# Weight rows of 136 columns, and activation tiles set 128 bytes from them modulo 256

## The chip, the cores and the metric

The kernel runs on one core of one Trainium2 chip. The metric is the time of one execution on the device in microseconds (us), the median of several executions. Of each kernel one execution was also recorded by the hardware profiler; all rows below come from that one.

## The reference

One inference step of a two-layer decoder trunk in float32, for 256 prompt tokens and 8 sample tokens (264 together), with 1024 model channels. Each layer does the following, cut to what matters here:

```python
h = rmsnorm(x, norm1)
z = h @ w_in                       # 1024 x 6400: attention, convolution, recurrence, gates
ya, yb, yc = branches(z, state)    # windowed attention, gated convolution, HGRN2 recurrence
mix = g[0] * (ya @ w_pa) + g[1] * (yb @ w_pb) + g[2] * (yc @ w_pc)
x = x + mix @ w_o                  # 1024 x 1024
h2 = rmsnorm(x, norm2)
x = x + square(relu(h2 @ w_up)) @ w_down   # 1024 x 4096 and 4096 x 1024
```

The products with `w_in`, `w_pa`, `w_pb`, `w_pc`, `w_o`, `w_up` and `w_down` read some 134 MB of weights over both layers. Shifted caches and new states are written out as well.

## The kernel before

All activations lie transposed: channels on the 128 partitions, the 264 tokens along the free dimension, one k tile for each 128 channels. An output tile of 128 channels is one **unit**: for each k tile three matmuls add up in one PSUM bank. Weights and activations are each split into a part that the type fp32r holds (`_hi`) and a rest (`_lo`), and the product of the two rests is dropped. In `unit` (line 688) a k tile is

```python
pe.matmul(out[:, 0:TOK], wh, rh, start=start and k == 0, stop=False)            # line 695
pe.matmul(out[:, 0:TOK], wh, rl, start=False, stop=False)                       # line 696
last = pe.matmul(out[:, 0:TOK], wl, rh, start=False, stop=stop and k == nk - 1) # line 697
```

`wh` and `wl` are a 128 x 128 block of `w_hi` and `w_lo`: these are the stationary operand and are loaded anew for each of the three. `rh` and `rl` are a k tile of 264 columns of `h_hi` and `h_lo` (or of `mix_hi`, `a_hi`, `y_hi` and their `_lo`), the moving operand. There are 6144 such matmuls: the units of `w_in` (stage "in"), the branches, then `w_o`, `w_up` ("up", 32 units a layer) and `w_down` ("down", 32 units a layer). An up unit goes over k tiles 0 to 7 of `h_hi`; a down unit over 8 of the 32 k tiles of `a_hi`, from k tile 0, 8, 16 or 24 on. The first 192 of the matmuls, up to about 32 us, are written out apart (lines 666 to 684) and follow the first loads.

Weights come in pairs of units by DMA from the SP queue into `raw`. ScalarE rounds a unit into `w_hi` (line 1043), VectorE subtracts into `w_lo` (line 1292); both tiles hold a ring of four units, and `w_used` tells when a slot is free. The first six splits write pieces of a pair, in runs of 128 columns (lines 1048 and 1298). VectorE and ScalarE also evacuate and norm; the attention and recurrence work of TensorE is put between units in small matmuls.

What the change touches is where tiles lie inside a partition. Tiles are laid one behind the other in the order of their declaration, each rounded up to 32 bytes. A k tile row of `w_hi` or `w_lo` has 128 x 4 = 512 bytes, a k tile of an activation 264 x 4 = 1056 bytes, which is 4 x 256 + 32. From the start of `w_hi` to that of `h_hi` are 16384 (`w_hi`) + 16384 (`w_lo`) + 8448 (`x`) = 41216 bytes, 161 x 256. Call **distance** the address of a moving k tile less that of the weight row that is used with it, modulo 256. It is then 0, 32, 64, ... 224 for k tiles 0 to 7 of `h_hi`, the same for `h_lo` (8448 bytes on, 33 x 256) and with `w_lo`. `mix_hi` and `a_hi` begin 32 further (76832 = 300 x 256 + 32 bytes from `w_hi`), so their distances run 32, 64, ... 224, 0; those of `y_hi` begin at 160.

Of the kernel before, what the change touches and what calls it, by code (L numbers as in the profile page):

```python
# [24 lines left out]
F32R = mybir.dt.float32r  # L25
# [5 lines left out]
P = 128  # L31
D_MODEL, DEPTH, PROMPT, SAMPLES, PAST = 1024, 2, 256, 8, 1024
TOK = PROMPT + SAMPLES
KT = D_MODEL // P
# [3 lines left out]
NG = len(GROUPS)  # L38
# [29 lines left out]

O_IN, O_O, O_UP, O_DN, OUTS = 0, 50, 58, 90, 98
RING = 4  # L70
PAIRS = UNITS // 2
LEVELS = [1, 2, 4, 8, 16, 32, 64, 128]

# [43 lines left out]
def slot(l, u):  # L117

    return (l * UNITS + u) % RING

# [6 lines left out]
def trunk(nc, io):  # L127
    with ExitStack() as ctx:
        def sb(name, shape, dt=F32, stack=ctx):
            return stack.enter_context(nc.sbuf_tensor(name, shape, dt))  # L130
# [3 lines left out]


        raw = sb("raw", [P, 3, KT, 2 * P])
        w_hi = sb("w_hi", [P, RING, KT, P], F32R)
        w_lo = sb("w_lo", [P, RING, KT, P], F32R)
        x = sb("x", [P, KT, TOK])
        h_hi = sb("h_hi", [P, KT, TOK], F32R)  # L140
        h_lo = sb("h_lo", [P, KT, TOK], F32R)
        consts = sb("consts", [P, NCONST])
# [13 lines left out]
        conv_in = sb("conv_in", [P, 3, 2 + PROMPT])  # L156


        with ExitStack() as early:
            gates = sb("gates", [P, N_GATE, TOK], stack=early)  # L160
            z = sb("z", [P, CT_GATE, TOK], stack=early)
            kv_tm = sb("kv_tm", [P, 2, NG, 2, P], stack=early)
            kv_s = sb("kv_s", [SAMPLES, NG, 2, P], stack=early)
            q_s = sb("q_s", [SAMPLES, NG, P], stack=early)
            kg = sb("kg", [P, 2, TOK], stack=early)
            v_tm = sb("v_tm", [P, 2, 2, P], stack=early)
            v_s = sb("v_s", [SAMPLES, 2, P], stack=early)
            o_c = sb("o_c", [P, 2, TOK], stack=early)
            y_a = sb("y_a", [P, TOK], stack=early)
            f_s = sb("f_s", [P, 2, SAMPLES], stack=early)  # L170
            state_p = sb("state_p", [P, 2, HD], stack=early)
            conv_s = sb("conv_s", [P, 3, SAMPLES, 2], stack=early)
            conv_u = sb("conv_u", [P, 3, SAMPLES], stack=early)
            conv_new = sb("conv_new", [P, 3, SAMPLES, 2], stack=early)
            q_heads = sb("q_heads", [P, NG, SAMPLES, 2], stack=early)
            sc = sb("sc", [P, NG, SAMPLES, 2], stack=early)
            pr_s = sb("pr_s", [P, NG, SAMPLES, 2], stack=early)
            s_rows = sb("s_rows", [2 * SAMPLES, NG * P + NG], stack=early)
            new_sc = sb("new_sc", [2 * SAMPLES, NG, SAMPLES], stack=early)
            s_stat = sb("s_stat", [2 * SAMPLES, 3], stack=early)  # L180
            new_pv = sb("new_pv", [P, NG, SAMPLES], stack=early)
            ya_new = sb("ya_new", [P, SAMPLES], stack=early)
            stat = sb("stat", [P, 2, 4], stack=early)
            s_att = sb("s_att", [P, 2 * P], stack=early)
            v_cache = sb("v_cache", [P, SAMPLES, NG, P], stack=early)

            with ExitStack() as s:
                cum_f = sb("cum_f", [P, 2, PROMPT], stack=s)
                suf_f = sb("suf_f", [P, 2, PROMPT], stack=s)
                q_lv = sb("q_lv", [P, 2, 2, PROMPT], stack=s)  # L190
                k_lv = sb("k_lv", [P, LV_SLOTS, 2, P], stack=s)
                att = sb("att", [P, 2, 4, P], stack=s)
                att_far = sb("att_far", [P, 2, 2, P], stack=s)
                k_tm = sb("k_tm", [P, 2, 2, P], stack=s)
                state_s = sb("state_s", [P, SAMPLES, 2, HD], stack=s)
            with ExitStack() as s:
                probs = sb("probs", [P, 2, 2, ROW_KEYS], stack=s)
                probs_t = sb("probs_t", [P, 4 * ROW_BLOCKS, P], stack=s)
            sb("shared_region", [P, 48 * P], stack=early)

            with ExitStack() as s:
                k_cache = sb("k_cache", [P, SAMPLES, NG, P], stack=s)
            y_hi = sb("y_hi", [P, BT, TOK], F32R, stack=early)
            y_lo = sb("y_lo", [P, BT, TOK], F32R, stack=early)
        with ExitStack() as s:
            sb("gates_below", [P, N_GATE, TOK], stack=s)
# [5 lines left out]
        a_lo = sb("a_lo", [P, FT, TOK], F32R)  # L212
        u_relu = sb("u_relu", [P, RING, TOK])
        a_full = sb("a_full", [P, RING, TOK])

        sample_parts = gates[:, 10:12, :].rearrange("p a t -> p (a t)")
        q_wide = sample_parts[:, 0:P].rearrange("p (a j m) -> p a j m", a=2, j=2)
# [182 lines left out]
        def raw_slot(p):  # L400

            return (p + 2) % 3 if p < U_UP // 2 else (p - U_UP // 2) % 2
# [20 lines left out]
        def raw_landings(l, p):  # L423

            slots = [raw_slot(q) for q in range(PAIRS)]
            return l * slots.count(raw_slot(p)) + slots[:p + 1].count(raw_slot(p)) - (raw_slot(p) in (raw_slot(0), raw_slot(1)))
# [222 lines left out]
        def _(pe):  # L649
# [26 lines left out]
            def unit_lo_last(u, out):  # L676

                pe.wait_ge(w_hi_ready, u + 1)
                for k in range(KT):
                    pe.matmul(out[:, 0:TOK], w_hi[:, u % RING, k, :], h_hi[:, k, :], start=k == 0, stop=False)  # L680
                    pe.matmul(out[:, 0:TOK], w_hi[:, u % RING, k, :], h_lo[:, k, :], start=False, stop=False)  # L681
# [1284 lines left out]
```

## Time and profile before

| | |
|---|---|
| median of 3 executions | 812.22 us (811.76 to 812.28) |
| span of the profiled execution, first to last instruction | 809.8 us |
| TensorE busy with matmuls | 801.3 us, 99% |
| VectorE, ScalarE, GpSimd busy | 70%, 54%, 34% |
| mean granted TensorE clock | 0.997 of full speed |
| HBM over the span | 300 GB/s |

The span of the profiled execution lies 2.4 us under the median, by the launch and the end of the program that it leaves out. "PE" is a matmul, "PEld" a weight load. A matmul's duration in a row (some 284 ns) runs from its start to its modelled end and overlaps the next one's; how fast the stream goes is read from the starts of matmuls that follow one another.

### The profile page before, as it was taken

To read this page: it belongs to the slowest core of one execution; us is meant where nothing else is said; L and a number is where in the kernel's file an instruction comes from. 1 tells how busy PE (TensorE), PEld (TensorE's weight loads), DVE (VectorE), ACT (ScalarE), POOL (GpSimd) and SP (SyncE) were. 2 spreads that over 40 slices of the span, in tenths; PEclk is the share of its full clock that TensorE was granted. 3 is DMA by queue.
4 is the path that set the end of the run, shared out by engine and by line. 5 is a ranking of instruction groups with operands and counts; after the bars stand their busy time and mean duration, and the time that the engine had idled before them with its cause. 6 is when DMAs were issued, how large, how long until landed. Compare 5 with 4: busy or idle time off the path is not lost.

```text
span 809.8 us, 17686 instructions
## 1 busy us (share of the span) xinstructions
PE 801.3 (99%) x6786; PEld 789.7 (98%) x6786; DVE 570.3 (70%) x774; ACT 439.6 (54%) x627; POOL 274.7 (34%) x246
## 2 busy tenths in 40 slices
PE   8999999999999999999999999999999999999996
PEld 8999999999999999999999999999999999999996
DVE  6978898577877665545577788966797666645552
ACT  6663667545557664444354637674455666644442
POOL 3599293055700000122149827702663000001220
PEclk9999999999999999999999999999999999999998
DMA  8797779868567688777558968986765767787751
GB/s 327 226 342 279 279 236 328 229 226 314 185 208 226 215 287 285 257 239 250 190 179 225 359 244 289 278 254 232 271 225 178 247 235 250 240 285 241 253 207 53
DMA packets 125721, 199.88 MB, mean 247 GB/s; under 512 B 19680, under 2 KB 115376, under 8 KB 118192
## 3 DMA queue, kind: packets, MB, share of 16 engines
q1 hardware_dynamic: 124368, 196.48, 72.3%
q10 hardware_dynamic: 1296, 2.61, 0.9%
q8 instruction: 39, 0.64, 0.3%
q14 instruction: 18, 0.15, 0.1%
HBM read 191.17 MB, written 51.90 MB: 300 GB/s over the span
## 4 chain that ended last, share of the span: by engine, by line
PE 98%; DVE 1%; DMA 1%; ACT 0%; DVEq 0%; ACTq 0%; issue 0%
PE main L695 29%; PE main L696 28%; PE main L697 28%; PE small L697 1%; PE small L696 1%; PE small L695 1%; PE small L711 1%; PE small L740 1%; PE small L754 1%; DMA raw<-in_w_in 1%; PE main L680 1%; PE main L681 0%; PE main L684 0%; PE small L792 0%; PE main L671 0%; PE small L928 0%
## 5 line engine op out<-in xcount | busy, mean ns | idle before, releaser
L1043 ACT ACTIVATE w_hi<-raw 128x1024 fp32r<-128x1024 f32 (+1 forms) x256 | 266.4, 1043 | 234.3 <-PE main L697 148.6
L1292 DVE TENSOR_TENSOR w_lo<-raw,w_hi 128x1024 fp32r<-128x1024 f32 (+1 forms) x256 | 340.8, 1332 | 65.5 <-ACT w_hi L1043 64.5
L695 PE MATMUL main<-h_hi,w_hi 128*128 128x264 f32 x1248 | 357.9, 287 | 0.0
L696 PE MATMUL main<-h_lo,w_hi 128*128 128x264 f32 x1248 | 354.0, 284 | 0.0
L697 PE MATMUL main<-h_hi,w_lo 128*128 128x264 f32 x1248 | 353.9, 284 | 0.0
L695 PEld LDWEIGHTS main<-h_hi,w_hi 128*128 128x128 f32 x1248 | 235.3, 189 | 3.0 <-DVE w_lo L1292 1.5
L696 PEld LDWEIGHTS main<-h_lo,w_hi 128*128 128x128 f32 x1248 | 235.5, 189 | 0.1
L697 PEld LDWEIGHTS main<-h_hi,w_lo 128*128 128x128 f32 x1248 | 234.2, 188 | 0.0
L695 PE MATMUL main<-a_hi,w_hi 128*128 128x264 f32 x512 | 145.4, 284 | 0.0
L697 PE MATMUL main<-a_hi,w_lo 128*128 128x264 f32 x512 | 145.2, 284 | 0.0
L696 PE MATMUL main<-a_lo,w_hi 128*128 128x264 f32 x512 | 145.2, 284 | 0.0
L696 PEld LDWEIGHTS main<-a_lo,w_hi 128*128 128x128 f32 x512 | 96.6, 189 | 0.0
L695 PEld LDWEIGHTS main<-a_hi,w_hi 128*128 128x128 f32 x512 | 96.5, 188 | 0.0
L697 PEld LDWEIGHTS main<-a_hi,w_lo 128*128 128x128 f32 x512 | 96.1, 188 | 0.0
L1698 POOL TENSOR_TENSOR sq_sum<-x 128x264 f32<-128x264 f32 x4 | 6.2, 1539 | 229.3 <-DVE x L1671 223.8
L1700 POOL TENSOR_TENSOR sq<-x 128x264 f32<-128x264 f32 x27 | 36.2, 1340 | 119.1 <-DVE x L1671 112.8
L1655 DVE SCALAR_TENSOR_TENSOR u_relu<-main,rstd 128x264 f32<-128x264 f32 x64 | 27.6, 431 | 33.5 <-PE main L697 32.6
L1259 ACT ACTIVATE a_full<-u_relu 128x264 f32<-128x264 f32 x64 | 27.1, 423 | 44.0 <-DVE u_relu L1655 43.4
L1323 DVE TENSOR_TENSOR gates<-main,rstd 128x264 f32<-128x264 f32 x48 | 20.5, 428 | 40.8 <-PE main L697 40.7
L1847 POOL TENSOR_TENSOR gated<-gated 128x264 f32<-128x264 f32 x14 | 18.2, 1303 | 86.5 <-DVE gated L1484 85.8
L1323 DVE TENSOR_TENSOR z<-main,rstd 128x264 f32<-128x264 f32 x52 | 22.1, 429 | 25.6 <-PE main L697 24.5
L695 PE MATMUL main<-mix_hi,w_hi 128*128 128x264 f32 x128 | 36.4, 284 | 0.0
(241 smaller groups left out, 1042.5 us busy)
## 6 DMA issues: line engine op xcount, KB each, us to landing
raw<-in_w_in SPq DMA_DIRECT2D x48, 1024.0 KB, 6.3
raw<-in_w_up SPq DMA_DIRECT2D x32, 1024.0 KB, 5.3
raw<-in_w_down SPq DMA_DIRECT2D x32, 1024.0 KB, 5.4
out_kvs<-in_cache SPq DMA_DIRECT2D x48, 512.0 KB
out_kvs<-in_cache SPq DMA_DIRECT2D x32, 496.0 KB
raw<-in_w_o SPq DMA_DIRECT2D x8, 1024.0 KB, 6.0
raw<-in_w_br SPq DMA_DIRECT2D x8, 768.0 KB, 4.8
gates<-q_scratch SPq DMA_DIRECT2D x4, 768.0 KB, 7.9
```

Of the source, the lines that this page charges most:

```text
L680: pe.matmul(out[:, 0:TOK], w_hi[:, u % RING, k, :], h_hi[:, k, :], start=k == 0, stop=False)
L695: pe.matmul(out[:, 0:TOK], wh, rh, start=start and k == 0, stop=False)
L696: pe.matmul(out[:, 0:TOK], wh, rl, start=False, stop=False)
L697: last = pe.matmul(out[:, 0:TOK], wl, rh, start=False, stop=stop and k == nk - 1)
L711: mm = pe.transpose(bank[0:n, col:col + k], src, ident[0:k, 0:k])
L1043: act.activation(w_hi[:, slot(l, u), 0:k, :], raw_of(u, k), ACT.Copy).then_inc(w_hi_ready, 1)
L1259: act.activation(a_full[:, j, :], u_relu[:, j, :], ACT.Square).then_inc(u_used, 1)
L1292: dve.tensor_tensor(w_lo[:, slot(l, u), 0:k, :], raw_of(u, k), w_hi[:, slot(l, u), 0:k, :].bitcast(F32), ALU.subtract).then_inc(w_lo_ready, 1)
L1323: dve.tensor_tensor(dst, main[bank_of(l, o)][:, 0:TOK], rstd[:, :], ALU.mult).then_inc(out_taken, 1)
L1655: dve.scalar_tensor_tensor(u_relu[:, j, :], main[bank_of(l, O_UP + j)][:, 0:TOK], 0.0, rstd[:, :], ALU.max, ALU.mult).then_inc(out_taken, 1)
L1700: step(pool.tensor_tensor(sq[:, :], x[:, k, :], x[:, k, :], ALU.mult))
L1847: step(pool.tensor_tensor(gated[:, s, 0, :], gated[:, s, 0, :], gated[:, s, 1, :], ALU.add))
```

## The change

Rows of the weight tiles get 8 columns (32 bytes) more, which nothing reads or writes: a k tile row is 544 bytes, 2 x 256 + 32, and a slot of eight is 4352 bytes, 17 x 256. Four unused tiles (`before_h`, `before_gates`, `before_y_hi`, `before_y_lo`) move the starts of `h_hi`, of `gates` (and with it `mix_hi` and `a_hi`, which begin where `gates` does or where the tile behind it does), of `y_hi` and of `y_lo`. From `w_hi` to `h_hi` are then 43392 bytes, 169 x 256 + 128; to `a_hi` 79232, 309 x 256 + 128; to `y_hi` 190080, 742 x 256 + 128. As a weight row and an activation's k tile now both step by 32 modulo 256, the distance is 128 for every k tile of every product; to the row of the next k tile it is 96. The three tiles of sample rows `kv_s`, `q_s` and `v_s` (8 partitions each) become parts of one tile at partitions 0, 64 and 32, which frees 2560 bytes a partition.

```diff
@@ -68,6 +68,7 @@
 RING = 4
+LINE = 8
@@ -134,9 +135,10 @@
         raw = sb("raw", [P, 3, KT, 2 * P])
-        w_hi = sb("w_hi", [P, RING, KT, P], F32R)
-        w_lo = sb("w_lo", [P, RING, KT, P], F32R)
+        w_hi_rows = sb("w_hi_rows", [P, RING, KT, P + LINE], F32R)
+        w_lo_rows = sb("w_lo_rows", [P, RING, KT, P + LINE], F32R)
         x = sb("x", [P, KT, TOK])
+        sb("before_h", [P, 4 * LINE])
         h_hi = sb("h_hi", [P, KT, TOK], F32R)
         h_lo = sb("h_lo", [P, KT, TOK], F32R)
@@ -156,15 +158,14 @@
+        sb("before_gates", [P, 7 * LINE])
         with ExitStack() as early:
             gates = sb("gates", [P, N_GATE, TOK], stack=early)
             z = sb("z", [P, CT_GATE, TOK], stack=early)
             kv_tm = sb("kv_tm", [P, 2, NG, 2, P], stack=early)
-            kv_s = sb("kv_s", [SAMPLES, NG, 2, P], stack=early)
-            q_s = sb("q_s", [SAMPLES, NG, P], stack=early)
+            sample_heads = sb("sample_heads", [P, NG * 2 * P], stack=early)
             kg = sb("kg", [P, 2, TOK], stack=early)
             v_tm = sb("v_tm", [P, 2, 2, P], stack=early)
-            v_s = sb("v_s", [SAMPLES, 2, P], stack=early)
@@ -200,7 +201,9 @@
+            sb("before_y_hi", [P, 4 * LINE], stack=early)
             y_hi = sb("y_hi", [P, BT, TOK], F32R, stack=early)
+            sb("before_y_lo", [P, 2 * LINE], stack=early)
             y_lo = sb("y_lo", [P, BT, TOK], F32R, stack=early)
@@ -212,6 +215,11 @@
+        w_hi, w_lo = (t[:, :, :, 0:P] for t in (w_hi_rows, w_lo_rows))
+        kv_s = sample_heads[0:SAMPLES, :].rearrange("p (g k c) -> p g k c", g=NG, k=2)
+        v_s = sample_heads[32:32 + SAMPLES, 0:2 * P].rearrange("p (a c) -> p a c", a=2)
+        q_s = sample_heads[64:64 + SAMPLES, 0:NG * P].rearrange("p (g c) -> p g c", g=NG)
```

Every engine's and queue's instructions stay the same in number and order. What differs in their shapes: the 256 splits on ScalarE and as many on VectorE, whose weight operands were one run of 1024 (or 768) columns, now go over 8 (or 6) runs of 128.

## Rows read from the trace of the kernel before

**Rows 1.** The page: engines, granted clock in 40 slices, the chain that ended last.
```profile
PE 801.3 (99%) x6786; PEld 789.7 (98%) x6786; DVE 570.3 (70%) x774; ACT 439.6 (54%) x627; POOL 274.7 (34%) x246
...
PEclk9999999999999999999999999999999999999998
...
PE 98%; DVE 1%; DMA 1%; ACT 0%; DVEq 0%; ACTq 0%; issue 0%
```

**Rows 2.** Groups by line and shape: the product's matmuls and the two splits.
```profile
L695 PE MATMUL main<-h_hi,w_hi 128*128 128x264 f32 x1248 | 357.9, 287 | 0.0
...
L697 PE MATMUL main<-h_hi,w_lo 128*128 128x264 f32 x1248 | 353.9, 284 | 0.0
...
L1292 DVE TENSOR_TENSOR w_lo<-raw,w_hi 128x1024 fp32r<-128x1024 f32 x240 | 322.5, 1345 | 65.5 <-ACT w_hi L1043 64.5 <-DVE cur L1439 0.2
L1043 ACT ACTIVATE w_hi<-raw 128x1024 fp32r<-128x1024 f32 x240 | 253.0, 1056 | 225.4 <-PE main L697 142.8 <-DMA raw<-in_w_down 50.5 <-DMA raw<-in_w_up 16.5
```

**Rows 3.** Waits of TensorE, two of five: us in total, times, longest.
```profile
PE small L654 <- DVE eps L1330: 1.5, 1, 1.5
...
PE main L671 <- DVE w_lo L1298: 0.4, 1, 0.4
```

**Rows 4.** Timeline of TensorE, one up unit: first matmul of each k tile.
```profile
230.89 0.28 PE L695 MATMUL main<-h_hi,w_hi 128*128 128x264 f32 x1
...
231.24 0.28 PE L695 MATMUL main<-h_hi,w_hi 128*128 128x264 f32 x1
...
231.61 0.29 PE L695 MATMUL main<-h_hi,w_hi 128*128 128x264 f32 x1
...
231.97 0.28 PE L695 MATMUL main<-h_hi,w_hi 128*128 128x264 f32 x1
...
232.33 0.28 PE L695 MATMUL main<-h_hi,w_hi 128*128 128x264 f32 x1
...
232.69 0.29 PE L695 MATMUL main<-h_hi,w_hi 128*128 128x264 f32 x1
...
233.06 0.28 PE L695 MATMUL main<-h_hi,w_hi 128*128 128x264 f32 x1
...
233.42 0.29 PE L695 MATMUL main<-h_hi,w_hi 128*128 128x264 f32 x1
...
233.79 0.28 PE L695 MATMUL main<-h_hi,w_hi 128*128 128x264 f32 x1
```

**Rows 5.** Timeline of TensorE: down stage of layer 0, four first matmuls and the last.
```profile
312.09 0.28 PE L695 MATMUL main<-a_hi,w_hi 128*128 128x264 f32 x1
...
314.26 0.29 PE L695 MATMUL main<-a_hi,w_hi 128*128 128x264 f32 x1
...
314.63 0.28 PE L695 MATMUL main<-a_hi,w_hi 128*128 128x264 f32 x1
...
314.98 0.28 PE L695 MATMUL main<-a_hi,w_hi 128*128 128x264 f32 x1
...
404.53 0.28 PE L695 MATMUL main<-a_hi,w_hi 128*128 128x264 f32 x1
```

**Rows 6.** Weight loads of 128 and of 64 columns, by line and shape.
```profile
L695 PEld LDWEIGHTS main<-h_hi,w_hi 128*128 128x128 f32 x1248 | 235.3, 189 | 3.0 <-DVE w_lo L1292 1.5 <-issue 0.2
...
L792 PEld LDWEIGHTS small<-probs_t,kv_tm 128*64 128x64 f32 x64 | 3.5, 137 | 0.3
```

**Rows 7.** The six splits that write runs of 128 columns: ns min/median/max.
```profile
L1048 ACT ACTIVATE w_hi<-raw x6: 617/632/1045, 5.4 to 12.8; 128x512 fp32r<-128x512 f32 x4, 128x1024 fp32r<-128x1024 f32 x2
...
L1298 DVE TENSOR_TENSOR w_lo<-raw,w_hi x6: 677/1155/1231, 6.0 to 15.5; 128x512 fp32r<-128x512 f32 x4, 128x1024 fp32r<-128x1024 f32 x2
```

**Rows 8.** Busy time by window: us, engine busy (x instructions), clock, DMA.
```profile
core 0: us, PE busy (x) PEld busy (x) DVE busy (x) ACT busy (x) POOL busy (x), PEclk, DMA share, GB/s
100.00:120.00 20.00, 20.00 (x167) 19.50 (x167) 19.93 (x20) 12.32 (x17) 19.60 (x13) 1.00 0.77 243
```

## The prediction

> **What bounds the kernel now.** I looked first for idle time of TensorE. There is next to none: it is busy 99% of the span, weight loads run for 98% of it, the clock is at its full level, 2.4 GHz, in all 40 slices but the last, and 98% of the chain that ended last is TensorE [rows 1]. Of its waits the longest, 1.5 us, is the start of the program, and the one for a split of weights comes to 0.4 us [rows 3]. So neither DMA, nor ScalarE or VectorE, nor a semaphore sets the time: the rate at which TensorE takes matmuls does. The next view is therefore one of starts. In the up stage of layer 0, k tile 0 of the fifth unit starts at 230.89 [rows 4]; 28 units and 672 matmuls later the down stage starts at 312.09 [rows 5]. That is 81.20 us, 2.900 us a unit, 120.83 ns a matmul. The 264 columns of a matmul, one a cycle at 2.4 GHz, would take 110.0 ns. The 10.8 ns between these two are what a change of layout can work on; over 6144 matmuls they are 66 us.
>
> The third view shows that they are not a fixed cost. Between the first matmuls of consecutive k tiles lie three matmuls, all with the same shapes, and yet 350 ns in one place and 370 ns in others [rows 4]. One unit is read to 10 ns only, so I took the starts of all 28 units from 230.89 to 312.09 and averaged each k tile's three steps. For k tiles 0 to 7 they take 355.5, 364.8, 365.2, 356.9, 358.1, 368.0, 361.0 and 370.5 ns, 362.5 in the mean. In the 32 units of the down stage (312.09 to 404.53 and the two matmuls after it [rows 5]) the same list comes out one place earlier: 363.3, 365.8, 356.7, 358.4, 367.2, 361.9, 370.0, 356.6. The row of 370 ns for instance, from 233.42 to 233.79, is k tile 7 in the up stage, and from 314.26 to 314.63 k tile 6 in the down stage. `a_hi` lies 32 bytes further from the weights than `h_hi`. So the cost goes neither with k, nor with the weight row's address, but with the activation's address modulo 256. By distance it is: 0, 356 ns; 32, 364; 64, 365; 96, 357; 128, 358; 160, 368; 192, 361; 224, 370.
>
> **Whether it is the distance.** In this kernel every weight row lies at the same address modulo 256, so the trace can't tell a conflict between two reads (which goes with the distance) from a property of the moving read alone (which goes with its address). Two things speak for the conflict. A weight load of 128 columns lasts 189 ns and one of 64 columns 137 [rows 6], so 64 columns take 52 ns and 128 some 104: the load of the next weights reads SBUF during almost the whole step of 121 ns, beside the moving operand. And 1056 bytes from any of the eight starting places touch five blocks of 256 bytes, nine of 128 and 17 of 64, so a read alone has the same number of blocks to fetch everywhere; nothing in it explains an order as uneven as 356, 364, 365, 357.
>
> **The change part by part.** *Rows of 544 bytes and the four shifts.* Today the eight distances come equally often in each product with 1024 rows, so the mean is 362.5 ns a triple. Afterwards every triple has distance 128, which today takes 358.1 ns (up) and 358.4 (down); I take 358.2. The load in its third step is of the next k tile's row, at distance 96, where third steps take 118.9 against 120.0 ns today; I take no credit for that. The gain is 4.3 ns a triple. Of the 2048 triples I leave out the first 64, which run until 32 us and are mixed with first loads; 1984 x 4.3 ns = 8.5 us. Both ends of this: at distance 128 the three steps are 118.1, 120.0 and 120.0 ns. The first of them follows another distance, which no longer happens. If all settle at the fast step, a triple is 354.3 and the gain 8.2 x 1984 = 16.3 us; if they settle at the mean of all second steps (whose neighbours before them have the same distance), 120.26 ns, the gain is 1.7 x 1984 = 3.4 us.
>
> *The splits.* 512 instructions write, and VectorE's also read, 8 runs of 128 columns where they had one of 1024. The nearest rows are the pieces at the start, which already write such runs: 1045 ns at most for 1024 columns on ScalarE, 1231 on VectorE [rows 7], against 1056 and 1345 for one run [rows 2]. So I take nothing for it, and the bounds lie at nothing too as long as it is hidden: ScalarE is busy 54% and VectorE 70% of the time, behind a ring of four units. The cover is thinnest at 100 to 120 us, where VectorE is busy 19.93 of 20 us and TensorE still 20.00 [rows 8]. Had VectorE there 5% more to do, it would fall 1 us behind, which comes twice (once a layer): 2 us. *Sample rows.* Their copies write the same few partitions' worth elsewhere; none is on the chain. *Small matmuls.* The other 642 matmuls get other distances as well; a triple today is at most 8 ns, 2.7 ns a step, off the mean, which gives 1.7 us either way; with no reason for a sign I take nothing. *Faster TensorE.* It now takes a unit in 2.866 us for 2.900. The splits need 1.35 us of VectorE and 1.06 of ScalarE a unit [rows 2], so the ring keeps up.
>
> Sum: 809.8 - 8.5 = 801.3 us for the profiled span; it lies 2.4 us under the median, so 803.7 us.
>
> **The rivals.** *No effect.* The cost goes with the moving operand's address alone. Its eight places modulo 256 still come equally often after the change, so the mean stays 362.5 ns and the time 812.2. The trace allows it, since weights never moved; the evenness of the block counts speaks against. The Trainium skill speaks for it: in "TensorE: Matmul & The Clock Gate", section "Step-by-step: what each phase is for", it says that TensorE has two independent SBUF read ports and that loading the next weights takes no read bandwidth from the running matmul. By that rule nothing is gained; that steps differ at all by address is something this rule doesn't explain. *A bad lock.* With one distance all through, each step starts in the state that the last one left, and it is the third steps today that come nearest to it. At distances 160, 192 and 224 these take 122.3, 123.1 and 122.3 ns, more than the mean of 120.83. If 128 settles there, 1.7 ns x 5952 matmuls are lost: 10 us, 822 us. It decides against the change from 121.1 ns a step on (0.27 ns are 1.6 us). Against it: the third step at 128 itself takes 120.0. *Late splits*, as priced above, would need both a gain of nothing and 2 us more: 814. *A cleaner stream.* The fastest step today is the second at distance 0, 116.0 ns. If no conflict at all leaves such a step everywhere, 4.8 ns x 5952 = 29 us are gained: 783 us. For it speaks that 10.8 ns a step are there; against, that distance 128 doesn't show it today.
>
> **How the numbers follow.** About 0.2% (1.6 us) can be told from no change. I give the forecast, from 795.9 to 808.8 us by the two ends above, 0.62; the cleaner stream 0.06; no effect 0.20; a bad lock 0.09; late splits 0.03. Faster is then 0.68, same 0.20, slower 0.12. The range goes from 795.5 to 813.0 us: it takes in the forecast and no effect, and leaves out 0.18.
>
> **What the profile after would show.** Right: starts of the first matmuls of k tiles 356 to 359 ns apart, the same for all eight and in the up and the down stage, a unit in 2.86 to 2.87 us; the split's durations within 2% of today's; still no wait of TensorE for a split beyond the first 32 us. If the list of eight values is found again, shifted to the new addresses of the activations, the moving operand's own address was the cause. If the eight are equal but near 362.5 or above, the distance counts and 128 is no good one. If units slow down only where VectorE is full, the splits are the cause. The prediction fails above all if steps settle at a value that the mixed distances of today don't show.

## The result, and the profile after

The changed kernel takes 813.88 us (median of 10, 813.16 to 820.94), the kernel before 811.87 us (median of 10, 811.48 to 812.28): ratio 1.0041, 95% interval 1.0021 to 1.006. It is slower, by some 2 us where a gain of 8.5 us was forecast. The profiled executions have spans of 811.4 and 809.8 us.

The page of the changed kernel answers to [rows 1]: engines, granted clock, chain.

```profile
PE 802.6 (99%) x6786; PEld 791.2 (98%) x6786; DVE 566.4 (70%) x774; ACT 439.8 (54%) x627; POOL 274.4 (34%) x246
...
PEclk9999999999999999999999999999999999999999
...
PE 98%; DVE 1%; ACT 0%; ACTq 0%; issue 0%; DVEq 0%
```

Nothing has moved off TensorE, and its clock is full. Groups by line and shape, against [rows 2] (line 695 is now 703, 697 is 705, 1292 is 1300, 1043 is 1051):

```profile
L703 PE MATMUL main<-h_hi,w_hi_rows 128*128 128x264 f32 x1248 | 358.0, 287 | 0.0
L705 PE MATMUL main<-h_hi,w_lo_rows 128*128 128x264 f32 x1248 | 356.5, 286 | 0.0
...
L1300 DVE TENSOR_TENSOR w_lo_rows<-raw,w_hi_rows 128x1024 fp32r<-128x1024 f32 x240 | 319.1, 1330 | 63.7 <-ACT w_hi_rows L1051 62.4 <-DVE cur L1447 0.2
L1051 ACT ACTIVATE w_hi_rows<-raw 128x1024 fp32r<-128x1024 f32 x240 | 253.2, 1056 | 225.6 <-PE main L705 148.0 <-DMA raw<-in_w_down 48.9 <-DMA raw<-in_w_up 15.0
```

The splits on VectorE and ScalarE take 1330 and 1056 ns where they took 1345 and 1056: writing 8 runs of 128 columns costs nothing. TensorE's waits (us in total, times, longest) are those of [rows 3]:

```profile
PE small L662 <- DVE eps L1338: 1.5, 1, 1.5
...
PE main L679 <- DVE w_lo_rows L1306: 0.4, 1, 0.4
```

So the steps themselves must have changed. This is the timeline of TensorE in the changed kernel at the place of [rows 4], the first matmul of each k tile in an up unit, then the first and the last of the down stage of layer 0:

```profile
232.37 0.28 PE L703 MATMUL main<-h_hi,w_hi_rows 128*128 128x264 f32 x1
...
232.73 0.28 PE L703 MATMUL main<-h_hi,w_hi_rows 128*128 128x264 f32 x1
...
233.09 0.28 PE L703 MATMUL main<-h_hi,w_hi_rows 128*128 128x264 f32 x1
...
233.45 0.28 PE L703 MATMUL main<-h_hi,w_hi_rows 128*128 128x264 f32 x1
...
233.81 0.28 PE L703 MATMUL main<-h_hi,w_hi_rows 128*128 128x264 f32 x1
...
234.17 0.28 PE L703 MATMUL main<-h_hi,w_hi_rows 128*128 128x264 f32 x1
...
234.53 0.28 PE L703 MATMUL main<-h_hi,w_hi_rows 128*128 128x264 f32 x1
...
234.89 0.28 PE L703 MATMUL main<-h_hi,w_hi_rows 128*128 128x264 f32 x1
...
235.25 0.28 PE L703 MATMUL main<-h_hi,w_hi_rows 128*128 128x264 f32 x1
...
313.19 0.28 PE L703 MATMUL main<-a_hi,w_hi_rows 128*128 128x264 f32 x1
...
405.21 0.28 PE L703 MATMUL main<-a_hi,w_hi_rows 128*128 128x264 f32 x1
```

All eight k tiles take 360 ns to the resolution of the rows; the averages of 28 units lie between 360.7 and 361.0. (Such averages come from the unrounded starts in the trace. The three matmuls of a k tile are called a triple.) From 232.37 to 313.19 are 80.82 us, 2.887 us a unit for 2.900, from unrounded starts; the down stage goes as fast. The up and the down stage thus did get faster, but the up stage starts at 232.37 us where it started at 230.89 [rows 4]. The 1.48 us were lost before it, in the stage of `w_in`: matched matmul by matmul, the changed kernel is 0.25 us ahead at 52.7 us of the kernel before and 1.54 us behind at 163.3. Up and down give 0.80 us back, since the last k tile of the down stage starts at 405.21 after 404.53 [rows 5]. What the in stage does shows in two of its stretches, first matmuls of k tiles again:

```profile
59.72 0.28 PE L703 MATMUL main<-h_hi,w_hi_rows 128*128 128x264 f32 x1
...
66.83 0.29 PE L703 MATMUL main<-h_hi,w_hi_rows 128*128 128x264 f32 x1
...
69.22 0.28 PE L703 MATMUL main<-h_hi,w_hi_rows 128*128 128x264 f32 x1
...
73.91 0.28 PE L703 MATMUL main<-h_hi,w_hi_rows 128*128 128x264 f32 x1
```

From 59.72 to 66.83 lie 19 k tiles, 374.2 ns each; from 69.22 to 73.91 lie 13, 360.8 ns each. Same lines, same tiles, same distance, and two speeds. Between the two stand small matmuls of the recurrence. Over the program, of 1217 triples on `h_hi` that no other matmul interrupts, 822 take 360 or 361 ns and 293 take 374 or 375. The same units are slow in both layers. Nearly every change of speed comes behind small matmuls, within the six triples after them, or at a product with other tiles.

Two changes of speed among these triples have no other matmul before them. The first product of layer 1 takes k tiles 0 to 6 of two units and only then k tile 7 of both. Behind k tile 6 of the first unit the next weight row to be loaded is that of k tile 0, at distance 64 for once in place of 96, and there the speed changes. These are first matmuls of k tiles 5 and 6, then of 0, 1 and 2 of the second unit, on the timeline of TensorE in the changed kernel:

```profile
407.37 0.28 PE L703 MATMUL main<-h_hi,w_hi_rows 128*128 128x264 f32 x1
...
407.73 0.28 PE L703 MATMUL main<-h_hi,w_hi_rows 128*128 128x264 f32 x1
...
408.10 0.29 PE L703 MATMUL main<-h_hi,w_hi_rows 128*128 128x264 f32 x1
...
408.46 0.29 PE L703 MATMUL main<-h_hi,w_hi_rows 128*128 128x264 f32 x1
...
408.84 0.29 PE L703 MATMUL main<-h_hi,w_hi_rows 128*128 128x264 f32 x1
```

Unrounded, these triples take 361, 363, 369 and 375 ns, and the next two 374. Between the two k tiles 7 the next row lies at 128 for once, and the triples go 375, 369, 361. In `w_o` (on `mix_hi`) the speed goes to 374 and back as well, at two breaks in the order of its k tiles. This speaks for the distance to the row that is loaded next having a part in the speed; it is not shown, as no run changes the order alone.

### The profile page after: what moved, and what is told of

The parts are those of the page before. It is cut to its first block, busy times and chain, and to the rows that moved or that the text cites. A ratio compares the mean times of both kernels' runs of the same rounds, so it can differ in the third digit from the quotient of the medians.

```text
span 811.4 us, 17686 instructions
## 1 busy us (share of the span) xinstructions
PE 802.6 (99%) x6786; PEld 791.2 (98%) x6786; DVE 566.4 (70%) x774; ACT 439.8 (54%) x627; POOL 274.4 (34%) x246
## 4 chain that ended last, share of the span: by engine, by line
PE 98%; DVE 1%; ACT 0%; ACTq 0%; issue 0%; DVEq 0%
PE main L703 29%; PE main L705 28%; PE main L704 28%; PE small L703 1%; PE small L704 1%; PE small L705 1%; PE small L719 1%; PE small L748 1%; PE small L762 1%; PE main L688 1%; PE main L689 0%; PE main L692 0%; PE small L800 0%; PE main L679 0%; PE small L936 0%; DVE h_lo L1316 0%
## 5 line engine op out<-in xcount | busy, mean ns | idle before, releaser
L1051 ACT ACTIVATE w_hi_rows<-raw 128x1024 fp32r<-128x1024 f32 (+1 forms) x256 | 266.7, 1043 | 234.9 <-PE main L705 152.4
L1300 DVE TENSOR_TENSOR w_lo_rows<-raw,w_hi_rows 128x1024 fp32r<-128x1024 f32 (+1 forms) x256 | 337.5, 1319 | 63.7 <-ACT w_hi_rows L1051 62.4
L703 PE MATMUL main<-h_hi,w_hi_rows 128*128 128x264 f32 x1248 | 358.0, 287 | 0.0
L705 PE MATMUL main<-h_hi,w_lo_rows 128*128 128x264 f32 x1248 | 356.5, 286 | 0.0
L704 PE MATMUL main<-h_lo,w_hi_rows 128*128 128x264 f32 x1248 | 354.5, 284 | 0.0
L703 PEld LDWEIGHTS main<-h_hi,w_hi_rows 128*128 128x128 f32 x1248 | 235.7, 189 | 3.0 <-DVE w_lo_rows L1300 1.5
L704 PEld LDWEIGHTS main<-h_lo,w_hi_rows 128*128 128x128 f32 x1248 | 234.7, 188 | 0.1
L705 PEld LDWEIGHTS main<-h_hi,w_lo_rows 128*128 128x128 f32 x1248 | 234.4, 188 | 0.0
L705 PE MATMUL main<-a_hi,w_lo_rows 128*128 128x264 f32 x512 | 145.9, 285 | 0.0
L703 PE MATMUL main<-a_hi,w_hi_rows 128*128 128x264 f32 x512 | 144.9, 283 | 0.0
```

What stands on the lines that cost most here:

```text
L1051: act.activation(w_hi[:, slot(l, u), 0:k, :], raw_of(u, k), ACT.Copy).then_inc(w_hi_ready, 1)
L1300: dve.tensor_tensor(w_lo[:, slot(l, u), 0:k, :], raw_of(u, k), w_hi[:, slot(l, u), 0:k, :].bitcast(F32), ALU.subtract).then_inc(w_lo_ready, 1)
```

## The experiments

**One theory** is that a step's time goes by the distance between the moving operand and the weights that are loaded beside it, that a stream of one distance settles in a state of its own, and that there may be more than one such state, chosen by how the stream begins (a stream, or stretch, is a run of such matmuls without others between). **Its rivals**: the moving operand's address alone counts; the rows of 544 bytes or the new places of other tiles cost the time; in the in stage other engines' accesses make the 374 ns.

**Rows of 512 bytes again, shifts kept.**

```diff
-        w_hi_rows = sb("w_hi_rows", [P, RING, KT, P + LINE], F32R)
-        w_lo_rows = sb("w_lo_rows", [P, RING, KT, P + LINE], F32R)
+        w_hi_rows = sb("w_hi_rows", [P, RING, KT, P], F32R)
+        w_lo_rows = sb("w_lo_rows", [P, RING, KT, P], F32R)
```

> Weight rows back at 512 bytes, the four shifts and the joint tile of sample rows kept: the distances are 128, 160, ... 96 for the eight k tiles, mixed as before. If the step goes by the distance and mixed distances average out: a unit is 2.900 us again in every stage, no stretch at 374 ns a triple, 812 us like the kernel before, with no execution above 814. If the shifts, the joint tile or the new places of other tiles cost the time: 813.9 us stays.

It took 811.62 us, ratio 0.9999 (0.9989 to 1.0009). Its first matmuls of the fifth up unit and of the down stage, on the timeline of TensorE:

```profile
230.91 0.28 PE L703 MATMUL main<-h_hi,w_hi_rows 128*128 128x264 f32 x1
...
312.11 0.28 PE L703 MATMUL main<-a_hi,w_hi_rows 128*128 128x264 f32 x1
```

These are 81.20 us for 28 units, to the hundredth what the kernel before has between 230.89 and 312.09. The averaged list of k tiles is 359, 367, 361, 371, 357, 363, 366, 356: the list of before, begun at its fifth place, where distance 128 stood. The joint tile of sample rows and the new places of everything else cost nothing; what changed the time is the rows of 544 bytes, by the constant distance that they bring or by themselves. The moved list doesn't tell distance from address, since all weight rows lie at one address modulo 256 again. The next runs decide between these.

**Other constant distances.** One line sets the distance of all products:

```diff
-        sb("before_h", [P, 4 * LINE])
+        sb("before_h", [P, 2 * LINE])
```

for 64 bytes; `3 * LINE` for 96, and so on; without the line it is 0. The change itself is the eighth distance, 128; the other seven:

> Rows of 544 bytes, all distances 0 in place of 128. If the stream settles by its distance: triples equal for all eight k tiles within a stretch, but at other values than 361 and 374 ns; from the triple of 356 ns that the kernel before has at distance 0, some 358 to 372. If the moving address alone counted: the eight values spread from 356 to 370 again and the time is 812. If rows of 544 bytes themselves cost the time: 361 and 374 as at distance 128, 813.9 us.

> All distances 64. By distance: one or two settled values, other than at 128; the kernel before has 365 ns a triple there, so rather slower, 365 to 380 ns and 816 to 830 us. By address alone or by the rows themselves: as for distance 0.

> All distances 96 (64 to the next k tile's row). By distance: the kernel before has 357 ns a triple there, the change's own good state 361; if the list of before tells the settled values at all, 357 to 361 ns and 803 to 809 us; if it doesn't, any value of 355 to 375 and two states as at 128. By address alone or by the rows themselves: as for distance 0.

> All distances 32. Settling by distance: all eight k tiles alike within a stretch, the value not to be had from the mixed list of before (364 ns a triple there): 64 gave 359.1 against 365 of the list, 96 gave 360.9 against 357, 128 gave 360.9 or 374.1 against 358. A time between 803 and 822 us. If the list counted: 364 ns, 815 us.

> All distances 160. Settling by distance: one or two values, 803 to 822 us; if the list of before counted (368 ns a triple): 823 us.

> All distances 192. Settling by distance: one or two values, 803 to 822 us; if the list of before counted (361 ns): 809 us.

> All distances 224. Settling by distance: one or two values, 803 to 822 us; if the list of before counted (370 ns): 827 us.

| distance | triple in the kernel before, ns | up unit at this distance alone, us | that is a triple of, ns | median, us | ratio (95% interval) |
|---|---|---|---|---|---|
| 0 | 356 | 2.913 | 364.2 | 815.77 | 1.0053 (1.0037 to 1.007) |
| 32 | 364 | 2.940 | 367.5 | 818.82 | 1.0071 (1.0048 to 1.0094) |
| 64 | 365 | 2.873 | 359.2 | 805.41 | 0.992 (0.9903 to 0.9936) |
| 96 | 357 | 2.887 | 360.8 | 808.58 | 0.9961 (0.9947 to 0.9976) |
| 128 (the change) | 358 | 2.887 | 360.8 | 813.88 | 1.0041 (1.0021 to 1.006) |
| 160 | 368 | 2.958 | 369.7 | 824.73 | 1.0159 (1.0142 to 1.0176) |
| 192 | 361 | 2.913 | 364.2 | 816.28 | 1.0054 (1.0038 to 1.0071) |
| 224 | 370 | 2.887 | 360.8 | 809.68 | 0.9971 (0.9961 to 0.9982) |

The up unit is read from the first matmul of the fifth up unit and of the down stage, as above; here for distances 0, 64, 96 and 160, each pair from the timeline of its own kernel.

```profile
231.80 0.28 PE L702 MATMUL main<-h_hi,w_hi_rows 128*128 128x264 f32 x1
...
313.37 0.28 PE L702 MATMUL main<-a_hi,w_hi_rows 128*128 128x264 f32 x1
```

```profile
229.26 0.28 PE L703 MATMUL main<-h_hi,w_hi_rows 128*128 128x264 f32 x1
...
309.71 0.28 PE L703 MATMUL main<-a_hi,w_hi_rows 128*128 128x264 f32 x1
```

```profile
230.65 0.28 PE L703 MATMUL main<-h_hi,w_hi_rows 128*128 128x264 f32 x1
...
311.48 0.28 PE L703 MATMUL main<-a_hi,w_hi_rows 128*128 128x264 f32 x1
```

```profile
234.02 0.28 PE L703 MATMUL main<-h_hi,w_hi_rows 128*128 128x264 f32 x1
...
316.83 0.29 PE L703 MATMUL main<-a_hi,w_hi_rows 128*128 128x264 f32 x1
```

These are 81.57, 80.45, 80.83 and 82.81 us for 28 units. Only the distance differs between these kernels (and the places of the tiles behind `before_h`, which alone cost nothing above), and the times go from 805 to 825 us: the rows of 544 bytes are not the cause, and the moving operand's address alone is not either, since its eight places come equally often in all eight kernels. In the expectations for 64, 96 and the four after them I had taken the list of before as a possible guide; it is no safe one. Five distances (32, 96, 128, 160, 192) settle 2 to 4 ns above their value in it, but it ranks 64 among the slow ones (365), where it is the fastest, 0 as the fastest (356), where it is slow, and 224 as the slowest (370), where it is fast. For 160 the 824.73 us lie outside the 803 to 822 that I expected and near the 823 by the list. The mean of the eight medians is 814.1 us, near the 811.9 of the mixed distances. Whether a distance has one speed shows in the in stage: at 64 its settled stretches all run at 359.0 to 359.4 ns a triple, at 96 at 360.7 to 360.9; at 0 some run at 367.5 beside 364, at 192 some at 374.1 beside 364, and at 32 they spread over 360.9 to 367.7. These are means: single triples of the up stage are alike to 1 ns only at 96 and 128. Elsewhere they repeat in a short pattern, at 32 for instance 366 and 369 ns in turn, at 80 (below) 364, 369 or 370, and 369. A pattern of three triples moves along the eight k tiles, so it doesn't belong to the activation's address.

**What chooses the state.** A matmul of another width ahead of each unit of the up loop, in the changed kernel; the unit overwrites its result:

```diff
                     for j in range(4):
                         pe.wait_ge(w_lo_ready, l * UNITS + i * 4 + U_UP + j + 5)
                         pe.wait_ge(out_taken, l * OUTS + i * 4 + O_UP + j + 1)
+                        n = (32, 64, 128, 200)[j]
+                        pe.matmul(main[bank_of(l, O_UP + j)][:, 0:n], w_hi[:, slot(l, U_UP + j), 0, :], h_hi[:, 0, 0:n],
+                                  start=True, stop=True)
                         unit(slot(l, U_UP + j), main[bank_of(l, O_UP + j)], h_hi, h_lo, 0, KT).then_inc(w_used, 1)
```

> The changed kernel (distance 128) with one more matmul ahead of each unit of the up loop, whose result is overwritten: 32, 64, 128 and 200 columns ahead of the four units of a turn. It costs some 56 x 0.1 = 6 us. If a stretch keeps the state in which its start has put it: units of the up stage are no longer all at 361 ns a triple; behind some of the four widths they run at 374, and the down stage, without such matmuls, at one of the two all through. If the 374 of the in stage comes from what other engines do there: the up stage stays at 361 behind all four.

It took 821.93 us, ratio 1.0124 (1.0104 to 1.0145). Timeline of TensorE in this kernel: line 1008 is the added matmul (128x32: 32 columns), line 703 the first of a k tile.

```profile
232.49 0.18 PE L1008 MATMUL main<-h_hi,w_hi_rows 128*128 128x32 f32 x1
232.52 0.37 PE L703 MATMUL main<-h_hi,w_hi_rows 128*128 128x264 f32 x1
...
234.44 0.29 PE L703 MATMUL main<-h_hi,w_hi_rows 128*128 128x264 f32 x1
...
234.81 0.29 PE L703 MATMUL main<-h_hi,w_hi_rows 128*128 128x264 f32 x1
...
235.19 0.29 PE L703 MATMUL main<-h_hi,w_hi_rows 128*128 128x264 f32 x1
...
235.56 0.19 PE L1008 MATMUL main<-h_hi,w_hi_rows 128*128 128x64 f32 x1
235.59 0.37 PE L703 MATMUL main<-h_hi,w_hi_rows 128*128 128x264 f32 x1
...
236.40 0.28 PE L703 MATMUL main<-h_hi,w_hi_rows 128*128 128x264 f32 x1
...
238.21 0.28 PE L703 MATMUL main<-h_hi,w_hi_rows 128*128 128x264 f32 x1
```

Behind 32 columns the last k tiles are 0.37 and 0.38 us apart; behind 64 the five from 236.40 to 238.21 take 0.362 each. Averaged over the 14 units of each width, the last two full triples of a unit take 374.0 and 374.4 ns behind 32 columns, 372.3 and 374.3 behind 128, 360.6 and 360.9 behind 64 and behind 200. The down stage, without added matmuls, runs at 360 or 361 ns in all its 511 triples. It is the same stage, with the same work on the other engines, and the start decides: the rival that other engines make the 374 ns falls.

The same at distance 64 (both edits above together):

> Distance 64 with the same additional matmuls of 32, 64, 128 and 200 columns ahead of the units of the up loop as at distance 128. If 64 is fast because it has one settled state, which every start falls into: behind all four widths the triples of a unit come back to 359.1 ns (mean of four) within the unit, and the time is 805.4 and some 6 us for the matmuls, 811. If 64 too has a slow state that the program's starts only happen to miss: behind at least one width the unit ends at 364 ns or more.

It took 812.07 us, ratio 1.0005 (0.9994 to 1.0016), 6.7 us more than distance 64 without the added matmuls. Behind 32 columns, in this kernel's timeline:

```profile
241.68 0.18 PE L1008 MATMUL main<-h_hi,w_hi_rows 128*128 128x32 f32 x1
241.71 0.37 PE L703 MATMUL main<-h_hi,w_hi_rows 128*128 128x264 f32 x1
...
242.87 0.28 PE L703 MATMUL main<-h_hi,w_hi_rows 128*128 128x264 f32 x1
...
244.31 0.28 PE L703 MATMUL main<-h_hi,w_hi_rows 128*128 128x264 f32 x1
```

The four k tiles from 242.87 to 244.31 take 0.360 each. Averaged over 14 units, the last four triples of a unit take 359.2 ns behind 32 columns, 359.0 behind 64, 359.0 behind 128 and 359.3 behind 200. At 64 I found one state only, at 128 two.

**Between the steps of 32 bytes.** The weights are written and read 4 columns (16 bytes) further in their rows, with activations at 96 (`3 * LINE` as above) for distance 80 and at 64 (`2 * LINE`) for 48:

```diff
-        w_hi, w_lo = (t[:, :, :, 0:P] for t in (w_hi_rows, w_lo_rows))
+        w_hi, w_lo = (t[:, :, :, 4:4 + P] for t in (w_hi_rows, w_lo_rows))
```

> Distance 80 for all tiles, by reading the weights 16 bytes further in their rows (columns 4 to 131) with activations at 96. If the settled time goes smoothly with the distance: between 64 (359.1 ns a triple, 805.4 us) and 96 (360.9, 808.6 us), or a little under both. If only blocks of 32 bytes count: as 64 or as 96.

> Distance 48: weights 16 bytes further in their rows, activations at 64. Smoothly with the distance: between 64 (805.4 us) and 32 (818.8 us). If blocks of 32 bytes count: as 32 or as 64.

Distance 80 took 817.58 us (1.0071, 1.0055 to 1.0088), distance 48 took 813.59 us (1.0024, 1.0014 to 1.0033). Distance 80 is slower than both its neighbours, 805.41 and 808.58, so both expectations for it were wrong; 48 lies between 64 and 32, as expected of a smooth course. At 80 again there are two speeds, 360.9 and some 367.5 ns a triple in the in stage, and the up stage has the slower one, 82.32 us for 28 units:

```profile
231.37 0.29 PE L703 MATMUL main<-h_hi,w_hi_rows 128*128 128x264 f32 x1
...
313.69 0.28 PE L703 MATMUL main<-a_hi,w_hi_rows 128*128 128x264 f32 x1
```

## Why the prediction was wrong

**What bounds the kernel** held: TensorE is busy 99%, waits for nothing that it didn't wait for before, and the whole difference lies in its steps.

**Whether it is the distance** held too: at the constant distance of 128 the eight k tiles became equal, in the up and the down stage alike, and the rival "no effect" fell. With rows of 512 bytes the list came back in the order of the new distances.

**The step that failed** is "afterwards every triple has distance 128, which today takes 358.1 ns". The list of before has each distance once, behind a triple at a distance of 32 less, and what a triple takes there says little of the time in which a stream of that one distance settles. The likely reason is that a triple starts in the state that the one before left. At 128 that is 360.8 ns or 374.1, by how the stretch began. At 360.8 the steps are 120.83, 118.33 and 121.67 ns in the mean; where the kernel before has 118.1, 120.0 and 120.0: the fast step is the second now, and the other two are above 120.0. The slow end that I had set, 120.26 ns a step, is that of the good state (120.28), as far as is known by chance. The gain where this state holds was therefore at the low end of what was forecast: 1.7 ns a triple, 0.80 us from the fifth up unit to the end of the down stage. And it holds in part of the stream only.

**The rival that came true** is the bad lock, and I gave it 0.09. It was priced for all stages, 10 us, at 1.7 ns a step; it held in part of the program, above all in the in stage, by 11.6 ns a triple (374.1 for 362.5). Matched with the kernel before, the 319 triples of 374 or 375 ns (293 of them on `h_hi`) cost 3.7 us, the 1477 of 360 or 361 give 2.5 back, the triples between the two states cost 0.5 and all the rest gains 0.2: that is the 1.5 us by which the span grew. That the third steps of before argued against it was the same mistake as above. The prediction's last sentence names this way of failing: no triple in the list of before takes 374 ns. That the time came out near the 812.2 of "no effect" is luck, as a loss and a gain nearly cancel.

**The splits, the sample rows and the ring** were priced at nothing and cost nothing: 1330 and 1056 ns, and shifts and joint tile alone gave a ratio of 0.9999.

What stays open: whether one of the two reads waits for the other, and which; why 374.1 is a state at 128 and was not found at 64; and what share the next k tile's row has. In every kernel with one distance that row's own distance is 32 less, 96 at distance 128. The prediction took no credit for this load, from third steps of 118.9 ns at 96 in the kernel before; here the third step takes 121.67. No run changes one of the two distances without the other. Two executions of the changed kernel took 820 and 821 us. An up and a down stage at 374.1 ns a triple would cost 512 x 13.3 ns = 6.8 us more than at 360.8, which fits, but no profile shows such an execution.

The version to keep is distance 64: 805.41 us, 0.8% under the kernel before and 1.0% under the change, with this one line of the change altered.

## What to carry to other kernels

When matmuls follow one another without a wait and still take unequal times by k tile, work out where the moving tile and the weight rows lie modulo 256, make the difference constant, and then measure every difference: the order of eight mixed ones doesn't tell the order of eight constant ones. Look also at the places where the order of k tiles breaks, since the next row comes from another distance there. Look for two speeds of the same line within one profile, since the median of a kernel that can settle either way depends on what stands ahead of each stretch. A stretch can keep the speed into which its start has put it, so add an interruption on purpose before you trust the fast one.

## What was not expected of the hardware

A stream of equal matmuls keeps one of two speeds, 360.8 or 374.1 ns a triple at distance 128, for as long as nothing else comes between and the k tiles keep their order: over 19 k tiles in the stretch shown, over the up and the down stage of a layer at 360.8. Sixteen bytes change the time by 1.1% to 1.5% (805.41 at distance 64, 817.58 at 80, 808.58 at 96). "TensorE: Matmul & The Clock Gate" of the Trainium skill, section "Step-by-step: what each phase is for", has weight loads take nothing from the running matmul's reads; the eight distances, with 805 to 825 us for the same instructions, don't agree with it.
